# Expert weights loaded as 16 KB runs per partition, token rows stored with their columns dealt to match

## What is computed

```python
x = x + jnp.concatenate([y_s5, y_hg], axis=-1) @ p['w_out']
x = x + _hier_moe(_rmsnorm(x, p['norm_ffn']), ...)      # then a final RMSNorm

def _hier_moe(x, w_coarse, b_coarse, w_fine, b_fine, w_gate, w_up, w_down):
    ...                              # top-1 of 4 groups, then top-2 of its 8 experts: gate (n, 32)
    hg = jnp.einsum('nd,edf->nef', xs, w_gate)          # w_gate, w_up: (32, 2048, 512)
    hu = jnp.einsum('nd,edf->nef', xs, w_up)
    act = jax.nn.silu(hg) * hu * gate.astype(x.dtype)[:, :, None]
    out = jnp.einsum('nef,efd->nd', act, w_down)        # w_down: (32, 512, 2048)
```

## Time and profile before

| | |
|---|---|
| median of 3 runs | 1862.39 us (1859.77 to 1868.12) |
| span of the profiled execution | 1859.5 us; the fastest run shown is 0.3 us above it, the median 2.9 us |
| TensorE matmul busy | 1491.5 us (80%) |
| TensorE weight load, VectorE, ScalarE, GpSimd busy | 845.5, 589.6, 274.7, 292.6 us |
| mean granted TensorE clock | 0.902 of full speed |
| DMA, whole span | 253053 packets, 505.25 MB |
| DMA in the chain that ended last | 35% of the span, TensorE 25% |

### The profile page before, as it was taken

The page is one execution under the profiler, slowest core; times in us unless marked ns, Lnnn a source line. Parts: engine busy times, 40 slices in busy tenths (PEclk is TensorE's granted clock), DMA queues, the critical chain, the costliest instruction groups (busy, mean ns, idle before and its releaser), DMA issues.

```text
span 1859.5 us, 19166 instructions
## 1 busy us (share of the span) xinstructions
PE 1491.5 (80%) x7437; PEld 845.5 (45%) x7437; DVE 589.6 (32%) x1466; ACT 274.7 (15%) x501; POOL 292.6 (16%) x402
## 2 busy tenths in 40 slices
PE   6898898879989996887777777878777788787780
PEld 5676666667757774432333333323333333333230
DVE  2789999856653223100100101001001001010015
ACT  2100001233330000110111111111111111111011
POOL 0055555433300000000000000000000000000006
PEclk9999899999998997998989999988988887899895
DMA  9333222433516444899999999999999999999964
GB/s 286 110 110 117 91 91 91 127 114 118 162 36 198 145 177 161 328 393 399 377 393 368 363 396 378 383 383 379 373 376 371 383 383 376 389 383 388 362 261 149
DMA packets 253053, 505.25 MB, mean 272 GB/s; under 512 B 23572, under 2 KB 99556, under 8 KB 233708
## 3 DMA queue, kind: packets, MB, share of 16 engines
q1 hardware_dynamic: 235788, 493.74, 73.7%
q0 software_dynamic: 5200, 9.19, 1.6%
q10 hardware_dynamic: 12016, 1.66, 0.6%
HBM read 503.18 MB, written 26.28 MB: 285 GB/s over the span
## 4 chain that ended last, share of the span: by engine, by line
DMA 35%; PE 25%; SPq 6%; DVE 1%; POOL 1%; issue 1%; ACT 0%; POOLq 0%; ACTq 0%; DVEq 0%
DMA ring<-in_w_up_dram 34%; PE bank L1254 16%; PE bank L1184 6%; SPq L378 6%; PE bank L1275 1%; PE bank L893 1%; DMA ring<-expert_rows 0%; PE bank L1151 0%; PE bank L1134 0%; POOL arena L855 0%; POOL arena L856 0%; PE bank L1162 0%; DVE arena L1791 0%; PE bank L1204 0%; PE bank L1221 0%
## 5 line engine op out<-in xcount | busy, mean ns | idle before, releaser
L1254 PE MATMUL bank<-ring,arena 128*64 128x512 f32 x2048 | 512.1, 656 | 149.1 <-DMA ring<-in_w_up_dram 149.1
L1254 PEld LDWEIGHTS bank<-ring,arena 128*64 128x64 f32 x2048 | 199.6, 150 | 434.6 <-issue 434.6
L1275 PE MATMUL bank<-ring,arena 128*64 128x512 f32 x1024 | 270.3, 689 | 19.0 <-DVE arena L1778 19.0
L1773 DVE SCALAR_TENSOR_TENSOR arena<-arena,gcol 64x512 f32<-64x512 f32 x32 | 23.8, 744 | 712.8 <-ACT arena L718 712.8
L923 PE MATMUL bank<-arena,ring 128*128 128x280 f32 x768 | 193.8, 413 | 4.0 <-ACT arena L573 2.6
L923 PEld LDWEIGHTS bank<-arena,ring 128*128 128x128 f32 x768 | 149.0, 196 | 47.5 <-issue 8.6
L1275 PEld LDWEIGHTS bank<-ring,arena 128*64 128x64 f32 x1024 | 83.2, 156 | 182.6 <-issue 182.6
L832 POOL DMA_INDIRECT expert_rows<-arena,idx_dst x32 | 29.5, 921 | 799.6 <-ACT arena L723 799.6
L723 ACT ACTIVATE arena<-bank 64x512 f32<-64x512 f32 x128 | 75.9, 593 | 342.5 <-PE bank L1275 341.4
L1184 PE MATMUL bank<-ring,arena 128*128 128x256 f32 x512 | 115.5, 387 | 0.0
L1221 PE MATMUL bank<-ident,arena 64*128 64x64 f32 x721 | 67.2, 242 | 57.6 <-DVE arena L1773 44.8
(11 more groups left out here) (333 smaller groups left out, 1406.9 us busy)
## 6 DMA issues: line engine op xcount, KB each, us to landing
ring<-in_w_down_dram SPq DMA_DIRECT2D x64, 2048.0 KB, 21.0
ring<-in_w_gate_dram SPq DMA_DIRECT2D x64, 2048.0 KB, 19.5
ring<-in_w_up_dram SPq DMA_DIRECT2D x64, 2048.0 KB, 22.6
ring<-in_w_in_dram SPq DMA_DIRECT2D x20, 2048.0 KB, 8.3
ring<-in_w_out_dram SPq DMA_DIRECT2D x8, 2048.0 KB, 9.5
ring<-in_s_w_glu_dram SPq DMA_DIRECT2D x2, 2048.0 KB, 8.3
arena<-v_samples SPq DMA_DIRECT2D x8, 512.0 KB, 4.3
ring<-expert_rows SPq DMA_DIRECT2D x4, 1024.0 KB, 9.1
```

Source lines behind the costliest of these rows:

```text
L1254: ins = pe.matmul(PB[b][at:at + CAP, :], xgT[b][:, kk, :], slot(s, KD // 2)[:, k, :], start=(kk == 0), stop=(kk == KD - 1))
L1275: ins = pe.matmul(PB[2 + cc // 2][at:at + CAP, :], hT[:, f, :], slot(4 + half, KF // 2)[:, k, cc * 512:(cc + 1) * 512], start=(f == 0), st ...
```

## The change

For the experts' weights, rows are dealt in another order. Partition p gets rows 16p to 16p + 15 of `w_gate` and `w_up`, and rows 4p to 4p + 3 of `w_down`, of which each load brings one half: 8 rows of 2 KB or 2 rows of 8 KB that follow each other in DRAM, one run of 16 KB. TensorE's k-th matmul thus meets row 16p + k where it met row 128k + p, and the other operand has to follow:

- the rows stored in `x1_rows` have their columns dealt, so that column 16q + k stands at 128k + q. GpSimd makes this copy of x1, 24 copies of 256 columns, in `xg0`, `xg1` and `yout[1]`, which are free at that time; SP stores from there and waits for `x1_dealt`;
- the gain is loaded once more in the dealt order, as `gain_ffn`, by a DMA on ScalarE's queue, and line 1748 (now 1762) multiplies by it;
- the gated product reads its operands with a stride of 4 elements and writes 4 runs of 128.

The diff, without the two lines that name the new semaphores:

```diff
+        gain_ffn = sb("gain_ffn", [P, KD])
...
+        x1_deal = [xg0, xg1, yout[1]]
...
             def load_gate_up(e, q):
                 w = t["w_gate"] if q % 2 == 0 else t["w_up"]
-                half = D // 2
-                src = w[0][bass.ds(e, 1), (q // 2) * half:(q // 2 + 1) * half, :]
-                sp.dma_start(slot(MOE_SLOT[q], KD // 2), src.rearrange("a (k p) n -> p (a k) n", p=P)) \
+                half = KD // 2
+                src = w[0][bass.ds(e, 1), :, :].rearrange("a (p k) n -> p (a k) n", p=P)
+                sp.dma_start(slot(MOE_SLOT[q], half), src[:, (q // 2) * half:(q // 2 + 1) * half, :]) \
                     .then_inc(slot_loaded[MOE_SLOT[q]], 16)
             def load_down(e, s):
-                half = FH // 2
-                src = t["w_down"][0][bass.ds(e, 1), (s - 4) * half:(s - 3) * half, :]
-                sp.dma_start(slot(s, KF // 2), src.rearrange("a (k p) n -> p (a k) n", p=P)) \
+                half = KF // 2
+                src = t["w_down"][0][bass.ds(e, 1), :, :].rearrange("a (p k) n -> p (a k) n", p=P)
+                sp.dma_start(slot(s, half), src[:, (s - 4) * half:(s - 3) * half, :]) \
                     .then_inc(slot_loaded[s], 16)
...
-            sp.wait_ge(x1_ready, 2 * NO)
+            sp.wait_ge(x1_dealt, 1)
             for tile in range(3):
-                sp.dma_start(x1_dram[tile * P:tile * P + TT[tile], :], x1[0:TT[tile], tile, :]).then_inc(x1_stored, 16)
+                sp.dma_start(x1_dram[tile * P:tile * P + TT[tile], :], x1_deal[tile][0:TT[tile], :]).then_inc(x1_stored, 16)
...
+            act.dma_start(gain_ffn[:, :], t["norm_ffn"].rearrange("a (p k) -> p (a k)", p=P)).then_inc(gain_loaded, 16)
...
+            for b in range(2):
+                pool.wait_ge(st_stored[b], 16 * NH // 2)
+            per = CB // KD
+            for o in range(NO):
+                for tile in range(3):
+                    n = TT[tile]
+                    pool.wait_ge(x1_ready, 2 * o + 1 + tile // 2)
+                    dealt = x1_deal[tile].rearrange("p (k q) -> p k q", k=KD)[0:n, :, o * per:(o + 1) * per]
+                    ins = pool.tensor_copy(dealt, x1[0:n, tile, o * CB:(o + 1) * CB].rearrange("p (q k) -> p k q", k=KD))
+            ins.then_inc(x1_dealt, 1)
             pool.wait_ge(x1_stored, 48)
...
+            dve.wait_ge(gain_loaded, 16)
...
-                              vecs[:, V_FFN + 8 * q:V_FFN + 8 * q + 8].unsqueeze(2).broadcast_to([P, 8, CAP]), ALU.mult)
+                              gain_ffn[:, 8 * q:8 * q + 8].unsqueeze(2).broadcast_to([P, 8, CAP]), ALU.mult)
...
-                        STT(hh[0:CAP, :], sg[0:CAP, :], gcol[b][:, 0:1], up[0:CAP, :], ALU.mult, ALU.mult).then_inc(h_made, 1)
+                        hk, sk, uk = (hh[0:CAP, :].rearrange("p (k q) -> p k q", k=KF),
+                                      sg[0:CAP, :].rearrange("p (q k) -> p k q", k=KF), up[0:CAP, :].rearrange("p (q k) -> p k q", k=KF))
+                        STT(hk, sk, gcol[b][:, 0:1], uk, ALU.mult, ALU.mult).then_inc(h_made, 1)
```

More of the change, by code:

```diff
@@ L285, in hymba_step @@
         fin_t, fin_read, fin_stored = sems("fin_t fin_read fin_stored")
-        x_again, out_done, x1_ready = sems("x_again out_done x1_ready")
+        x_again, out_done, x1_ready, gain_loaded, x1_dealt = sems("x_again out_done x1_ready gain_loaded x1_dealt")
         squares_ready, r_sum, r_rms, x1_stored, xt2_done, xt2_copied = sems(
```

## The result

The changed kernel takes **1835.9 us** (median of 4 runs, 1835.4 to 1839.5) against 1861.7 before (4 runs): ratio 0.985, 95% interval 0.9835 to 0.987. It is faster, by 26 us. The forecast was 1801 us; the range of 1784 to 1845 holds the result, but less than half of the forecast gain arrived. The profiled execution took 1835.85 us, its span is 1834.0.

The account below looks back on a forecast made before the run. The weight-load DMA queue was taken to bound the kernel, at 34.0 us an expert. 1859.5 - 62 (loads) + 0.6 (gain_ffn) = 1798 us profiled, with 2.9 more for the median 1801 us; range 1784 to 1845.

Parts of the forecast that it names:

- Landing gaps: Weight-load queue: a load takes 4.93 us instead of 5.4 (gate, up) or 5.0 (down); 62 us saved.
- half-gain rival: Weight loads: only half of the 0.4 us between gaps is due to piece size; 25 us gained, 1838; chance 12%.
- sum by the Trainium skill: Weight loads: about 3 cycles overhead a packet, 2 KB pieces some 3.5% slower than 8 KB; some 28 us, about 1835.
- Packets: Weight loads: 122,880 packets fewer, seven of eight for w_gate and w_up, half for w_down.
- Issues: SP queue: load issues of 0.4 us, where one w_up issue held it 10.88 us; counted as nothing.
- What comes late next: Expert stage: the DMA queue stays the longest loop at 32.0 us; GpSimd's loop needs 29.9, TensorE about 29.
- The GpSimd loop binds: Expert stage: 16 KB pieces add 1.6 us each to gather and scatter; turn 33.1, about 1835 us; chance 17%.
- slower rival: Expert stage: gathers and scatters wait in proportion to piece length; GpSimd loop 37.7 us, about 1977; chance 8%.
- Dealing and `gain_ffn`: Before the experts: GpSimd's copies cost 0, at most 3 us; the gain's DMA on ScalarE's queue +0.6, at most +3.9.
- The strided product: Line 1773, in TensorE's loop: the same or twice its 0.744 us; costs 0, at most 0.7 once.
- Rate: DMA engines over the expert stretch: 405 GB/s instead of 381.

Follow-up runs that it names:

- e11: Changed kernel plus 24 matmuls that nobody reads on TensorE, behind the gate and up product; 1821.8 us, ratio 0.980.
- e7: Changed kernel with the w_down load in 8 KB pieces and the product of line 1789 as before the change; 1850.7 us, ratio 0.993.
- e4: Changed kernel without the dealing of the residual rows, gain_ffn and the strided product, so expert sums differ; 1835.5 us, ratio 0.984.
- e1: Changed kernel with GpSimd issuing the next gather right behind the scatter instead of after it has landed; 1807.5 us, ratio 0.969.

## Why the prediction was wrong

**Landing gaps: right.** 4.93 us forecast, 4.89 measured; 4 KB pieces, at 5.12, lie on the line drawn between 2 and 8 KB. The half-gain rival falls. So does the sum by the Trainium skill ("DMA: Bandwidth & Descriptors", Why small descriptors are slow), whose 3 cycles a packet make 3.5% between 2 and 8 KB: the rows show 5.39 against 4.97, 8%. Its 1835 us hit the time by another mechanism.

**Packets: right.** 253053 - 130318 = 122,735 fewer, against 122,880. **Issues: right**, 0.33 to 0.38 us.

**The step that failed is "What comes late next".** It held the GpSimd loop at 29.9 us while it changed the pieces beside that loop. The turn of 29.9 us had this down product in it (kernel before, start us, us):

```profile
789.35 8.78 PE L1275 MATMUL bank<-ring,arena 128*64 128x512 f32 x32 [0.59 <-DVE arena L1778]
```

By the rows: 29.9, + 1.6 for the gather (9.0 for 7.4), - 0.5 for the scatter, + 1.25 for the transposes at the low clock, + 0.45 for the down product (busy 268.0 us in 29 turns, 9.24 each, for 8.78) = 32.7 us; measured 32.9. Against the 32.0 of the forecast, 31 x 0.9 = 28 us are missing, of 1835.9 - 1801 = 35. The rest lies at the ends: with the short first and last turns, the table's turn fell by 33.6 - 32.7 = 0.9 us where 2.02 were forecast, which makes some 34 us, and the first scatter was issued 1.8 us later (775.2 for 773.4). The transfers alone (29.9 + 1.6 - 0.5 = 31.0) would have stayed under the queue's turn; the 1.7 us at the lower clock, at which no step of the prediction looked, carry the loop past it. They can't be had apart, though: in e11, with most of the clock back, the scatter is 1 us longer and the turn still 32.2 of the 32.7 us, so the clock's net part of the 35 us is about 31 x 0.54 = 17 by the turn and 9 to 14 by the time.

**The rival "The GpSimd loop binds" was the case, at 17%**: 1835 us, a gather 1.6 us longer, and TensorE waiting for rows at each expert, as its sign was written down. That its time came out is in part luck: it had 1.6 us more in the scatter, which did not grow, and nothing for the clock, which cost 1.7. What I held against it, one gather of 8.7 us beside 2 KB pieces, was read wrongly. By its own numbers it landed at 1003.8 + 8.7 = 1012.5, 1.6 us after the last 2 KB load, so it did not run wholly beside 2 KB pieces; and it compared 2 with 8 KB, where nothing changes (7.4 to 7.5 us; 8.8 and 8.6 in the new order), and said nothing of 16 KB (9.0, and 11.1). The slower rival (waits in proportion to the piece) fails for the same reason: from 2 to 8 KB there is no growth at all. The Trainium skill ("DMA: Bandwidth & Descriptors", Queues, rings and completion order) says that an engine takes its queues in turn by whole packets. If a packet grows with the piece, the rows agree with that at 16 KB alone (9.0 us for 7.5) and not below (7.3 to 7.5 from 2 to 8 KB).

**Dealing and `gain_ffn`: right, small.** The copies take 0.61 us each, `gain_ffn` holds the queue 0.60 us (GpSimd's copies in the last stretch before the first gather, by line; ScalarE's queue):

```profile
L817 POOL COPY arena<-arena 128x256 f32<-128x256 f32 (+1 forms) x3 | 1.8, 613 | 15.8 <-DVE arena L1650 15.8
```

```profile
43.40 0.60 ACTq L555 DMA_DIRECT2D gain_ffn<-in_norm_ffn_dram  x1
```

The first gather started at 735.2 us, 2.8 later than before, but this start lies anywhere from 733.1 (e7) to 735.2 in kernels with the same dealing, and e4, without it, had it at 734.0, so it prices nothing of the change. **The strided product** went from 744 to 1113 ns, inside the bounds, and hides beside the transposes' wait.

**Rate.** 405 GB/s were forecast over the stage. The changed kernel reaches 391, at a DMA share of 0.97 instead of 1.03: its loads are issued late, as the row of 1030.70 above shows. That isn't all of it, since e1, where the queue binds, has 394 at the same share.

## What to carry to other kernels

When an edit makes the longest loop faster, work out the next loop again with the edit in it: its transfers share the hardware with those that were changed, and a loop of 29.9 us beside a new bound of 32.0 is not far off. A piece size that is best for the big transfers need not be best for the kernel: 8 KB gave away 1.6% of the load rate (4.97 for 4.89 us) and gained 25.7 us in the old order, and 16 KB paid only once gather and scatter no longer stood in series. And a wait on TensorE can cost more than its length: behind the waits of the changed kernel the transposes took 3.03 us instead of 1.78, at the lower clock.

## What the runs showed that I had not expected

- A gather of 64 rows takes the same beside pieces of 2, 4 and 8 KB (7.3 to 7.5 us) and 1.5 us more beside 16 KB. Why the step lies there was not settled: the 16 KB loads also skip every other 16 KB of DRAM, and no kernel with 16 KB pieces in one stretch was run.
- Work that nobody needs made the kernel 9 to 14 us faster (e11), by keeping TensorE busy where it had waited: the granted clock was 0.94 over the stage instead of 0.85.
- Transfers that got longer made the kernel faster: e1, with gathers of 11.1 us and scatters of 8.9, is the fastest of all, 1807.5 us, 3.1% under the kernel before. Smaller pieces for `w_down` alone made it slower (e7), in the old order by 15 us; the cause was not found.
